# Rotary partners by SBUF transfers in place of a rotation matmul, and one attention output in three split passes

## The reference, cut to what matters

```python
def apply_rope(t, cos, sin):                       # block one, head width 64
    t1, t2 = jnp.split(tf, 2, axis=-1)
    return jnp.concatenate([t1 * cos - t2 * sin, t2 * cos + t1 * sin], axis=-1)

def apply_rope_2(t, cos, sin):                     # block two, head width 128
    t0, t1 = tf[..., 0], tf[..., 1]                # even and odd elements
    out = jnp.stack([t0 * c - t1 * s, t0 * s + t1 * c], axis=-1)

q = apply_rope_2(split_heads_norm(q, q_norm[layer], N_HEADS), cos, sin)
k = apply_rope_2(split_heads_norm(k, k_norm[layer], N_KV_HEADS), cos, sin)
attn = latent_attention(q, k, v, kc, vc)
x_mix = merge_branches(attn, hyo, g, w_o_attn[layer], w_o_hyena[layer], w_out[layer])
    # merge_branches: ... g_attn * (attn_out @ w_o_attn) ...
```

## Time and profile before

| | before |
|---|---|
| median of three runs | 2564.53 us (2562.9 to 2566.35) |
| the profiled execution | 2564.82 us |
| its span in the profile | 2562.9 us |
| TensorE busy | 2502.8 us, 98% |
| POOL busy | 1426.0 us, 56% |
| ACT busy | 1234.4 us, 48% |
| DVE busy | 1153.3 us, 45% |
| DMA traffic | 347.63 MB, mean 136 GB/s |

### The profile page before, as it was taken

One profiled execution on the slowest core, in us unless ns is written; L12 is line 12 of the kernel. 1 busy time (PEld: TensorE's weight loads), 2 busy tenths in 40 slices (PEclk: granted clock), 3 DMA queues, 4 the chain that ended last, 5 costly groups with the idle time before them and its releaser, 6 DMA issues.

```text
span 2562.9 us, 42007 instructions
## 1 busy us (share of the span) xinstructions
PE 2502.8 (98%) x16580; PEld 2165.0 (84%) x16580; DVE 1153.3 (45%) x2172; ACT 1234.4 (48%) x2097; POOL 1426.0 (56%) x819
## 2 busy tenths in 40 slices
PE   7999999999999999999999999999999999999998
PEld 7998989888999888998677766778888878898998
DVE  8895645444977655537425512321101123535224
ACT  6467654455446764436553411443323346636543
POOL 6875746456976655455533122645565546464970
PEclk9999999999999999999999999999999999999999
DMA  6543343345544343345421111232222233235554
GB/s 247 182 169 136 132 164 141 140 170 185 189 165 158 139 152 144 132 149 190 176 72 61 50 66 66 103 113 84 99 99 85 97 115 120 83 143 185 192 183 148
DMA packets 50600, 347.63 MB, mean 136 GB/s; under 512 B 5360, under 2 KB 8688, under 8 KB 8944
## 3 DMA queue, kind: packets, MB, share of 16 engines
q1 hardware_dynamic: 47840, 340.31, 36.6%
q10 hardware_dynamic: 2576, 4.72, 0.6%
HBM read 343.96 MB, written 1.05 MB: 135 GB/s over the span
## 4 chain that ended last, share of the span: by engine, by line
PE 91%; DVE 3%; ACT 3%; issue 1%; POOL 1%; DMA 1%; ACTq 0%; DVEq 0%; SPq 0%; POOLq 0%
PE pg L1943 23%; PE pg L1945 23%; PE pg L1944 23%; PE pg L1968 2%; PE ps L2267 2%; PE pg L1966 2%; PE ps L2288 2%; PE ps L2286 1%; PE ps L2426 1%; PE ps L2407 1%; PE ps L2116 1%; ACT ring_hi L776 1%; PE ps L2122 1%; PE ps L2088 1%; PE ps L2507 1%
## 5 line engine op out<-in xcount | busy, mean ns | idle before, releaser
L661 POOL TENSOR_TENSOR ring_lo<-ring,ring_hi 128x1024 fp32r<-128x1024 f32 (+3 forms) x494 | 1148.6, 2339 | 745.9 <-ACT ring_hi L776 744.5
L1943 PE MATMUL pg<-HH,ring_hi 128*128 128x256 f32 (+1 forms) x3360 | 1076.4, 320 | 21.7 <-DVE HL L1325 8.5
L1944 PE MATMUL pg<-HH,ring_lo 128*128 128x256 f32 (+1 forms) x3360 | 1025.3, 305 | 0.0
L1945 PE MATMUL pg<-HL,ring_hi 128*128 128x256 f32 (+1 forms) x3104 | 953.1, 307 | 0.0
L1943 PEld LDWEIGHTS pg<-HH,ring_hi 128*128 128x128 f32 x3360 | 638.2, 190 | 96.3 <-issue 38.3
L1944 PEld LDWEIGHTS pg<-HH,ring_lo 128*128 128x128 f32 x3360 | 638.2, 190 | 46.7 <-issue 18.4
L1945 PEld LDWEIGHTS pg<-HL,ring_hi 128*128 128x128 f32 x3104 | 589.3, 190 | 30.5
L776 ACT ACTIVATE ring_hi<-ring 128x1024 fp32r<-128x1024 f32 (+6 forms) x564 | 555.4, 1002 | 32.3 <-DMA ring<-in_w_stream_dram 27.8
L786 ACT ACTIVATE take<-pg 128x256 f32<-128x256 f32 (+1 forms) x242 | 103.8, 429 | 471.0 <-PE pg L1945 418.9
L1945 PE MATMUL pg<-big_r,ring_hi 128*128 128x256 f32 (+1 forms) x864 | 274.0, 317 | 0.0
L1943 PE MATMUL pg<-big_r,ring_hi 128*128 128x256 f32 (+1 forms) x736 | 239.7, 326 | 3.9 <-DVE ring_lo L1632 2.7
(11 more groups left out here) (332 smaller groups left out, 3198.0 us busy)
## 6 DMA issues: line engine op xcount, KB each, us to landing
ring<-in_w_stream_dram SPq DMA_DIRECT2D x320, 1024.0 KB, 4.8
hn<-in_consts_dram ACTq DMA_DIRECT2D x2, 1024.0 KB, 6.1
cst<-in_consts_dram SPq DMA_DIRECT2D x1, 1472.0 KB, 19.8
prm<-in_params_dram SPq DMA_DIRECT2D x1, 1110.0 KB, 9.5
X<-in_xT_dram SPq DMA_DIRECT2D x1, 1024.0 KB, 5.6
X<-in_ctxT_dram ACTq DMA_DIRECT2D x1, 1024.0 KB, 7.2
out_dram<-H ACTq DMA_DIRECT2D x4, 256.0 KB, 2.2
cst<-in_consts_dram SPq DMA_DIRECT2D x1, 768.0 KB, 16.8
```

The costliest lines, as they stand in the source:

```text
L661: pool.tensor_tensor(ring_lo[:, slot, cols], ring[:, slot, cols], ring_hi[:, place * P:(place + n) * P].bitcast(F32), SUB).then_inc(sem(LO ...
L1943: first = pe.matmul(out, a[0], b[0], start=start, stop=False)
L1944: pe.matmul(out, a[1], b[0], start=False, stop=False)
L1945: return first, pe.matmul(out, a[0], b[1], start=False, stop=stop)
```

## The change

It does two things.

**Partner rows by transfers.** The rotation matmuls and their matrix are gone. ACT's queue issues DMAs inside SBUF that write the rows with partitions exchanged into free buffers: in block one four transfers of 32 partitions by 2048 columns for each half of the rows (`turn_qk`; the first half behind the emptying of `qk` chunk 8, the second behind value chunk 0), into `hn` and `sq`; in block two two transfers, even partitions to odd and odd to even (`turn2`), for the key heads behind query chunk 3, for query heads 0 to 3 behind value chunk 0, and for heads 4 to 7 behind hyena chunk 0. The sign that the matrix held goes into the sine tables. DVE's sine product now reads the partner rows and the sine from SBUF and writes the PSUM bank.

**Three passes.** The odd `oa` chunks of block two's layer 0 become split chunks like all others. The weights get eight more splits. The attention's output gets a high half (an ACT copy of 128x512 per head, `attention2_high`) and a low half (a POOL subtraction) per head during and behind the attention, as layer 1 already has it with 128x256.

The diff, cut to its core:

```diff
@@ -56,28 +56,17 @@
     c["levels"] = np.concatenate(lv, 1)
-    rot1 = np.zeros((P, P))
-    for d in range(P):
-        if d % QK_DIM < QK_DIM // 2:
-            rot1[d + QK_DIM // 2, d] = -1.0
-        else:
-            rot1[d - QK_DIM // 2, d] = 1.0
-    c["rot1"] = rot1
+    c["spare"] = np.zeros((P, P))
     c["tab1"] = np.zeros((P, 2 * T))
-    rot2 = np.zeros((P, P))
-    for d in range(0, P, 2):
-        rot2[d + 1, d] = -1.0
-        rot2[d, d + 1] = 1.0
-    c["rot2"] = rot2
     t = np.arange(T)
...
     c["cos2"] = np.repeat(np.cos(ang).T, 2, 0)
-    c["sin2"] = np.repeat(np.sin(ang).T, 2, 0)
+    c["sin2"] = np.repeat(np.sin(ang).T, 2, 0) * np.where(i % 2 == 0, -1.0, 1.0)[:, None]
     inv1 = 10000.0 ** (-np.arange(0, QK_DIM, 2, dtype=f) / QK_DIM)
-    c["inv1"] = np.tile(inv1, 4)[:, None]
+    c["inv1"] = np.concatenate([-inv1, inv1, -inv1, inv1])[:, None]
     tt = np.linspace(0.0, 1.0, T)[:, None]
@@ -333,8 +322,6 @@
-    if name == "oa" and l == 0:
-        return i % 2 == 0
     return name not in ("mod", "modt")
@@ -507,6 +496,7 @@
         MG = H[:, :, T:2 * T]
+        QK_TURNED = [hn[:, :], sq]
         AT_S = cut(at_buf, 0, 2, 2 * T)
@@ -545,7 +535,11 @@
         VX = cut(big, 10240, KH, 2 * T)
-        A2H, A2L = (cut(big_r, 0, HEADS, 2 * T)[:, :, s] for s in (slice(T, 2 * T), slice(0, T)))
+        A2L = cut(big_r, 0, HEADS, 2 * T)
+        A2H = [[cut(hn_r, 2 * T * h, 2 * T) for h in range(4)] + [cut(big_r, 12288 + 2 * T * h, 2 * T) for h in range(2)]
+               + [rows_r[:, h, :] for h in range(2)], [A2L[:, h, T:2 * T] for h in range(HEADS)]]
+        K2_TURNED = cut(big, 12288, 2, T)
+        Q2_TURNED = [cut(big, 10240 + 4 * T * h, 4, T) for h in range(2)]
         X0L, X0H = cut(big_r, 6144, KH, 2 * T), cut(big_r, 10240, KH, 2 * T)
@@ -580,7 +574,7 @@
         IT2_BASE = [0, len(IT2[0])]
-        HIGH_AT = [NT * h + NT + LAG + 1 for h in range(HEADS - 1)]
+        HIGH_AT = [[NT * n * (h + 1) + LAG + 1 for h in range(HEADS - 1)] for n in N_SEQ]
         DQ_N, DK_N, ATT_N, DO_N = (0, 1), (2, 3), 4, 5
@@ -733,12 +727,12 @@
                 n = N_TOK[l]
-                for h in range(HEADS if l == DEPTH - 1 else 0):
-                    done = whole(sum(att2_fill(l)[:(HIGH_AT + [ATT_STEPS + LAG])[h] + 1], []))
+                for h in range(HEADS):
+                    done = whole(sum(att2_fill(l)[:(HIGH_AT[l] + [STEPS2[l] + LAG])[h] + 1], []))
                     if done:
                         ahead(CHUNK[done[-1]])
-                    pool.wait_ge(sem("a2_high"), h + 1)
-                    pool.tensor_tensor(A2L[:, h, :], Q2_[:, h, 0:T], A2H[:, h, :].bitcast(F32), SUB).then_inc(sem("a2_low"), 1)
+                    pool.wait_ge(sem("a2_high"), HEADS * l + h + 1)
+                    pool.tensor_tensor(A2L[:, h, 0:n], Q2_[:, h, 0:n], A2H[l][h].bitcast(F32), SUB).then_inc(sem("a2_low"), 1)
                 for m in range(KD):
@@ -893,6 +887,19 @@
                 norm_root(i)
+
+            def turn_qk(l, half):
+
+                act.wait_ge(sem("drained"), DRAINED["qk", l, 8 * half + 7])
+                for a, b in ((0, 32), (32, 0), (64, 96), (96, 64)):
+                    act.dma_start(QK_TURNED[half][a:a + 32, :], big[b:b + 32, 2048 * half:2048 * (half + 1)])\
+                        .then_inc(sem(f"qk_turned{half}"), 16)
+
+            def turn2(name, dst, src, normed):
+
+                act.wait_ge(sem("hn_done"), normed)
+                for a, b in ((0, 1), (1, 0)):
+                    act.dma_start(dst[a:P:2], src[b:P:2]).then_inc(sem(name), 16)
@@ -1044,8 +1051,12 @@
                     drain(CHUNK["qk", l, j], QK[:, j, :])
+                    if j == 8:
+                        turn_qk(l, 0)
                 for j in range(8):
                     drain(CHUNK["v", l, j], V[:, j % 2, (j // 2) * T:(j // 2 + 1) * T])
+                    if j == 0:
+                        turn_qk(l, 1)
                 def dn_silu(j):
@@ -1168,10 +1179,10 @@
-            def attention2_high(h):
-
-                act.wait_ge(sem("a2_out"), IT2_BASE[DEPTH - 1] + NT * (h + 1))
-                act.activation(A2H[:, h, :], Q2_[:, h, 0:T], ACT.Copy).then_inc(sem("a2_high"), 1)
+            def attention2_high(l, h):
+
+                act.wait_ge(sem("a2_out"), IT2_BASE[l] + NT * N_SEQ[l] * (h + 1))
+                act.activation(A2H[l][h], Q2_[:, h, 0:N_TOK[l]], ACT.Copy).then_inc(sem("a2_high"), 1)
@@ -1200,13 +1211,19 @@
                         hn_square(Q2_[:, j - 3:j + 1, 0:n])
+                    if j == 3:
+                        turn2("k2_turned", K2_TURNED, K2_[:, :, 0:T], i + 1)
                     if j == 5:
...
                     drain(CHUNK["v2", l, j], V2_[:, j, :], n=2 * P)
+                    if j == 0:
+                        turn2("q2_turned0", Q2_TURNED[0], Q2_[:, 0:4, 0:T], i + 2)
                     if j == 2:
                         hn_root(i + 2, 4 * n, 1.0 / P)
-                drain_fill([("hy2", l, j) for j in range(EARLY_HY)])
+                drain_fill([("hy2", l, 0)])
+                turn2("q2_turned1", Q2_TURNED[1], Q2_[:, 4:8, 0:T], i + 3)
+                drain_fill([("hy2", l, j) for j in range(1, EARLY_HY)])
                 steps = IT2[l]
@@ -1214,10 +1231,9 @@
                         attention2_turned(IT2_BASE[l] + k - LAG, steps[k - LAG][1])
-                    if l == DEPTH - 1 and k in HIGH_AT:
-                        attention2_high(HIGH_AT.index(k))
-                if l == DEPTH - 1:
-                    attention2_high(HEADS - 1)
+                    if k in HIGH_AT[l]:
+                        attention2_high(l, HIGH_AT[l].index(k))
+                attention2_high(l, HEADS - 1)
                 gaps = iter(hyena_fill(l))
@@ -1648,13 +1664,12 @@
             dve.tensor_reduce(lam[:, 0:4], lqp.rearrange("p (a d) -> p a d", a=4), AX.X, ADD).then_inc(sem("lam_dots"), 1)
-            def rope(i, qk, cos, sin):
+            def rope(i, qk, other, cos, sin):
                 if i:
                     dve.wait_ge(sem("rope"), i)
-                dve.wait_ge(sem("rot"), i + 1)
                 dve.tensor_tensor(cut(at_buf, 0, 2, T), qk, rep(cos, 2), MUL).then_inc(sem("rope_cos"), 1)
                 turned = ps[:, 2 + i % 2, :].rearrange("p (a b) -> p a b", a=2)
-                link(dve.tensor_tensor(turned, turned, rep(sin, 2), MUL))
+                link(dve.tensor_tensor(turned, other, rep(sin, 2), MUL))
                 dve.wait_ge(sem("rope_cos"), i + 1)
@@ -1700,7 +1715,12 @@
                         dve.wait_ge(sem("rope_table"), 1)
-                rope1 = lambda jj: rope(8 * l + jj, QK[:, 2 * jj:2 * jj + 2, :], tab[:, 0, :], tab[:, 1, :])
+                def rope1(jj):
+
+                    dve.wait_ge(sem(f"qk_turned{jj // 4}"), 64 * (l + 1))
+                    other = QK_TURNED[jj // 4][:, jj % 4 * 2 * T:(jj % 4 + 1) * 2 * T].rearrange("p (a b) -> p a b", a=2)
+                    rope(8 * l + jj, QK[:, 2 * jj:2 * jj + 2, :], other, tab[:, 0, :], tab[:, 1, :])
+
                 for jj in range(ROPES_V):
@@ -1815,7 +1835,13 @@
             def rope2(l, jj):
-                rope(ROPE2[l] + jj, Q2_[:, 2 * jj - 2:2 * jj, 0:T] if jj else K2_[:, :, 0:T], C("cos2"), C("sin2"))
+
+                dve.wait_ge(sem(("k2_turned", "q2_turned0", "q2_turned1")[(jj + 1) // 2]), 32 * (l + 1))
+                if jj:
+                    qk, other = Q2_[:, 2 * jj - 2:2 * jj, 0:T], Q2_TURNED[(jj - 1) // 2][:, (jj - 1) % 2 * 2:(jj - 1) % 2 * 2 + 2, :]
+                else:
+                    qk, other = K2_[:, :, 0:T], K2_TURNED
+                rope(ROPE2[l] + jj, qk, other, C("cos2"), C("sin2"))
@@ -2052,9 +2078,8 @@
                     return chunk_parts(name, l, i, KH, parts_of(X0H, X0L, n), n)
-                if l == 0:
-                    return chunk_parts(name, l, i, KD, rows_of(Q2_, n), n)
-                return chunk_parts(name, l, i, KD, parts_of(A2H, A2L, n), n, low_ready("a2_low", 0) if i == 1 else None)
+                return chunk_parts(name, l, i, KD, lambda c: (A2H[l][c], A2L[:, c, 0:n]), n,
+                                   low_ready("a2_low", HEADS * l) if i == 1 else None)
@@ -2334,23 +2351,12 @@
                     chunk("qk", l, i, KD, hx, T)
-                rot1 = lambda jj: rot(8 * l + jj, C("rot1"), QK[:, 2 * jj:2 * jj + 2, :])
                 for part in range(4):
...
                         tokens_first("v", l, 2 * part + tt, w, tt, T, freed if tt == 0 else 0)
-                    if part == 1:
-                        pe.wait_ge(sem("drained"), DRAINED["qk", l, 15])
-                        if l == 0:
-                            pe.wait_ge(sem("rope_table"), 1)
-                            pe.wait_ge(sem("tables"), 32)
-                    if part in (1, 2):
-                        rot1(2 * part - 2)
-                        rot1(2 * part - 1)
                 for i in range(24):
-                    if i in (1, 2, 5, 6):
-                        rot1(ROPES_V + (1, 2, 5, 6).index(i))
```

(12 more changed lines are left out.)

14 lines of the change are left out of this document (5 added, 9 removed).

## The result

| | before | after |
|---|---|---|
| median of six runs each | 2565.01 us | 2575.3 us (2572.4 to 2578.06) |
| ratio, 95% interval | | 1.0041 (1.0031 to 1.0051) |
| the profiled execution, its span | 2564.82, 2562.9 | 2576.81, 2575.0 |
| sum of TensorE's waits (the rows of that view, added up) | 52.3 | 80.0 |
| us lost to a granted clock under 1.00 | 13.6 | 27.2 |

The change makes the kernel slower by 0.4%, where a gain of 20.1 was forecast; the difference to the forecast is 30.6. The last two rows of the table are of the profiled execution. The last one is added up from busy times in stretches of 4 us, ahead of the last 30 us: each gives 4 x (1 - granted clock). (A granted clock of 1.00 is 2.4 GHz, of 0.50 the lower level, 1.2 GHz.)

A forecast was written before the change was run, and what follows sets the result against it. TensorE, busy 98% of the span, was taken as the bound. Gains 22.4 + 10.2 less 2.2, 6.8, 2.2, 0.8 and 0.5 gave 20.1, so 2564.8 - 20.1 = 2544.7 us, range 2536 to 2558.

The forecast's parts named there:

- the side to which I gave 0.06: Whole kernel: the chance given to the change measuring slower than before; faster had 0.87, same 0.07.
- Removed rotations, 22.4: TensorE: 26 rotation matmuls go, 0.86 us each, a gain of 22.4 us.
- Output chunks, 10.2, less 0.5 for ACT: Block two, layer 0: eight attention-output chunks gain 1.28 us each, 10.2; added ACT copies cost 0.5.
- The sine product inherits nothing: I take an extra d of 0: Ropes on DVE: the sine product directly behind the cosine product keeps the SBUF path, so takes 0 us extra.
- d: Extra us per sine product on DVE once it reads two SBUF tensors; taken as 0, bounds 0 and 2.38.
- rival 4: Ropes: POOL runs a whole split behind each cosine product, 2.38 us per sine product; 26.2 less gain, 2570.9 us; chance 0.05.
- Block one's wait, 1.1 + 4d a layer: Deltanet stage: TensorE's chunk 10 waits for DVE's short convolutions, 1.1 + 4d us a layer, 2.2 in both.
- it still keeps up: Block one, 136 to 182: POOL, working 35.1 of 46.0 us, absorbs 0.69 lost per rope; no cost taken.
- Value stages, 6.8: Block two: TensorE waits for query-head ropes behind late transfers, 3.7 us in layer 0 and 3.1 in layer 1.
- Key rope in layer 1, 2.2: Block two, layer 1: TensorE waits 2.2 us for the key rope, whose transfers land about 2137.2.
- Start of attention, 0.8: Block two, layer 1: attention waits for ropes of query heads 4 to 7, 0.8 us, between 0 and 1.7.
- my own formula: Whole kernel: the gain is 20.1 - 11d us, for eleven ropes where a longer sine product counts.

The follow-up runs named there:

- three waits: The kernel before plus idle DVE multiplications, three each ahead of short convolutions 6, 8 and 10 in each layer of block one; 2574.0 us.
- single-part kernels: The kernel before with one part of the change: block one's transfers, 2578.6 us; block two's transfers, 2573.6 us; three passes, 2554.9 us.
- after, early transfers: The changed kernel, block two's key-head transfers issued behind query chunk 2 and those of query heads 0 to 3 behind query chunk 6; 2563.3 us.

## Why the prediction was wrong

Forecast 2544.7 with a range of 2536 to 2558; measured 2575.3, slower, on the side to which I gave 0.06. By its steps:

- **Removed rotations, 22.4:** right as far as the matmuls go; they are gone, and nothing takes their place.
- **Output chunks, 10.2, less 0.5 for ACT:** right; 10.6 alone, chunks 5.6 apart.
- **"The sine product inherits nothing: I take an extra d of 0":** this step failed. Measured is d = 1.23 in block one (1.92 - 0.69). The mechanism was that of rival 4, at half its price: 9 of 16 sine products in block one lost the path to a whole POOL split, the other seven nothing. I had drawn the rule from one merged row of another kind of operation, against the Trainium skill's statement (SBUF — State Buffer, "SBUF: two separate sides") of an exclusive lock that is held for one instruction. The sine product's 2.91 beside a POOL split agrees with it; three splits that kept POOL out for 2.5 aren't explained by it. The edit that takes the product's second SBUF input away is worth 19.4.
- **Block one's wait, 1.1 + 4d a layer:** with the measured d this is 6.0, and TensorE waited 1.07 + 4.94 = 6.0 for the short convolutions in layer 0 and the same in layer 1. The form was right, d was not, and the exact match is in part luck: of the four ropes that the formula counts two in each layer lost the path, 4.4 in all, which gives 5.5. Two waits on low halves of 1.7 and 1.9 were not in it: "it still keeps up" was true of the sum of POOL's work, not of the splits behind ropes 2 and 3.
- **Value stages, 6.8:** 4.32 + 2.36 = 6.7. The mechanism was right, that the sum fits is luck: 3.7 and 3.1 were forecast. In layer 0 the two transfers went beside a weight load and landed in 4.2 (3.5 taken), in layer 1 in 3.0; with block two's transfers alone the same two waits were 2.5 and 3.7.
- **Key rope in layer 1, 2.2:** 4.0, mis-sized; the two transfers of 128 KB landed 5.2 behind their issue, beside a weight load, and 2.1 in the kernel that issues them earlier.
- **Start of attention, 0.8:** 2.1, mis-sized.
- **The clock was in no term,** and this step failed too: I took every wait at its length. But the profile of before had the case: behind TensorE's wait of 3.9 at 627.8 its granted clock was 0.50 for 4 us. Of the seven new or longer waits of over 2 six took it down (not the 2.1 at attention's start), and those of 1.1 to 1.9 sometimes: 13.6 more in all. The wait (timeline of PE) and the stretches of before:

```profile
627.82 0.58 PE L1943 MATMUL pg<-HH,ring_hi 128*128 128x256 f32 x1 [3.90 <-DVE HL L1325]
```

```profile
624.00:628.00 4.00, 0.18 (x1) 0.18 (x2) 2.13 (x5) 2.99 (x6) 3.49 (x2) 0.88 0.97 395
628.00:632.00 4.00, 4.00 (x19) 4.00 (x20) 4.00 (x12) 2.94 (x7) 0.00 (x0) 0.50 0.71 274
```

Together: 32.6 - 27.7 - 13.6 = -8.7, against 12.1 that the span grew. 3.4 are left over, of which the eight further waits at 0.26 each may be 2 (an estimate from the row of "three waits"); in the single-part kernels what is left over is 2.8 (block one) and 0.3 (block two).

The range failed for the same two reasons: its upper bound took d only up to 0.73, and nothing for the clock. With d = 1.23 my own formula gives 2544.7 + 13.5 = 2558.2, the edge of the range, and with the clock 2572.

## What to carry to other kernels

A kernel whose matrix engine is busy 98% of the time isn't made faster by taking work off it if a queue behind it becomes later: price the operands' new home first (here two SBUF inputs on DVE beside a busy POOL cost up to a whole POOL split, 2.2, per operation), and change the place of an operand before the engine. Price each new wait of TensorE in one piece (here 2.4 to 4.9 us) at its length, and at 1.7 or 3.4 us more for the clock behind it. Where a transfer takes the place of a matmul, issue it at the moment its source is complete, not where the matmul stood: here that was worth 12 us for the first two groups. Then measure: the third group, issued earlier, lost 4.9.

## What the runs showed of the hardware

- A DVE product with two SBUF inputs and a POOL split shut each other out, and POOL can get in between two directly successive DVE operations: 2.85 to 2.91 for a sine product of 0.69, some 0.5 behind the end of the POOL split, whether it writes PSUM or SBUF; with one input in PSUM all 24 took 0.69. Three DVE splits in a row did keep a POOL operation out for 2.5, which stays unexplained.
- A transfer inside SBUF of 256 KB took 5.1 and 4.8 from and to 32 partitions (8 KB in a row each), and 3.0 from and to every second of 128 partitions in pieces of 1 KB (4.2 beside a weight load). The more scattered one was not the slower; but the first kind goes in bursts of four, the second of two, and no run separates the two differences.
- Eight plain sums of squares of 128x512 took 3.60 to 3.70 at a granted clock of 1.00 and 5.4 to 6.0 behind a wait of 2.5 to 4.3, where it was 0.55 to 0.88. Behind the 2.6 at 335 in "after, early transfers" it stayed at 1.00, and they took 3.70.
- Where the granted clock fell behind a wait of TensorE, it cost 1.7 or 3.4 us beyond the wait: behind each of the waits of 3.3 to 4.9 in these profiles, behind most of 2.2 to 2.7, in none of seven behind the 2.1 at the start of attention.
